# A chunked scan: the triangular inverse built from pairs X and U = X Aᵀ, one 128-column product per level

## What is computed

```python
def wkv_scan(state, r, w, k, v, a, b, reverse):
    def step(s, inp):
        r_t, w_t, k_t, v_t, a_t, b_t = inp
        sa = jnp.einsum('bhij,bhj->bhi', s, a_t)
        s = s * w_t[:, :, None, :] + sa[..., None] * b_t[:, :, None, :] + v_t[..., None] * k_t[:, :, None, :]
        return s, jnp.einsum('bhij,bhj->bhi', s, r_t)
```

## Time and profile before

| | |
|---|---|
| median of 3 runs | 2158.53 us (2154.55 to 2166.66) |
| profiled execution, its own time | 2158.71 us |
| its span in the profile | 2156.9 us |
| PE busy over the span | 1983.1 us |
| scan, about | 1190 to 2010 us of the span |
| PE busy in that stretch | 718.85 of 820 us |
| DVE, ACT, POOL busy in that stretch | 519.94, 345.90, 325.01 us |

### The profile page before, as it was taken

One profiled execution on the slowest core, in us unless ns is written; L12 is line 12 of the kernel. 1 busy time (PEld: TensorE's weight loads), 2 busy tenths in 40 slices (PEclk: granted clock), 3 DMA queues, 4 the chain that ended last, 5 costly groups with the idle time before them and its releaser, 6 DMA issues. The chain is left out here.

```text
span 2156.9 us, 64929 instructions
## 1 busy us (share of the span) xinstructions
PE 1983.1 (92%) x28556; PEld 1318.3 (61%) x28556; DVE 1120.8 (52%) x2187; ACT 701.5 (33%) x1985; POOL 541.3 (25%) x669
## 2 busy tenths in 40 slices
PE   6999999999999999999898788888889888988698
PEld 3556556344444454544343688888888888888443
DVE  4534333124756592042442566656666666766684
ACT  4111111133335642221012344344444444444332
POOL 1011010013113430002111433334434343434011
PEclk9999999999999999999999899999999999999899
DMA  8200000811016767546432333443333333332742
GB/s 345 103 20 25 34 20 20 347 63 49 22 55 167 203 176 206 154 151 202 156 112 80 96 84 92 127 115 85 98 86 100 87 96 88 100 99 64 242 135 100
DMA packets 269820, 248.24 MB, mean 115 GB/s; under 512 B 92770, under 2 KB 226146, under 8 KB 266083
## 3 DMA queue, kind: packets, MB, share of 16 engines
q1 hardware_dynamic: 269538, 244.09, 37.2%
HBM read 164.32 MB, written 79.69 MB: 113 GB/s over the span
## 5 line engine op out<-in xcount | busy, mean ns | idle before, releaser
L2173 PE MATMUL ps<-M,AT 64*64 64x64 f32 x6400 | 278.6, 222 | 37.3 <-issue 32.2
L1019 PE MATMUL ps<-xt,w_slab 128*128 128x512 f32 (+1 forms) x800 | 297.5, 525 | 0.0
L2173 PEld LDWEIGHTS ps<-M,AT 64*64 64x64 f32 x6400 | 234.7, 136 | 49.8 <-issue 37.8
L2173 PE MATMUL ps<-TT,MT 64*64 64x64 f32 x5120 | 223.7, 222 | 23.9 <-issue 21.6
L1019 PEld LDWEIGHTS ps<-xt,w_slab 128*128 128x128 f32 x800 | 148.3, 190 | 146.3 <-issue 122.6
L2173 PEld LDWEIGHTS ps<-TT,MT 64*64 64x64 f32 x5120 | 195.5, 136 | 29.6 <-issue 25.6
L2037 DVE COPY_PREDICATED TT<-mask,ps 128x128 f32<-128x128 int32 x400 | 130.2, 325 | 149.4 <-PE ps L2173 141.3
L1905 POOL TENSOR_TENSOR bk<-feat,growth 128x256 f32<-128x256 f32 x160 | 117.2, 754 | 348.2 <-ACT growth L1950 348.2
L2163 PE MATMUL ps<-ar,bk 64*64 64x192 f32 (+1 forms) x1280 | 133.2, 320 | 20.8 <-POOL ar L1915 14.3
L645 PE MATMUL ps<-h,fgo 128*128 128x512 f32 x320 | 142.7, 600 | 2.4 <-PEq L202 2.4
L2166 PE MATMUL ps<-ar,bk 64*64 64x192 f32 (+1 forms) x1280 | 134.1, 327 | 1.2 <-issue 1.2
(11 more groups left out here) (299 smaller groups left out, 4060.3 us busy)
## 6 DMA issues: line engine op xcount, KB each, us to landing
feat<-feature_scratch SPq DMA_DIRECT2D x160, 256.0 KB
feature_scratch<-k_feats SPq DMA_DIRECT2D x64, 320.0 KB, 5.1
feature_scratch<-k_feats SPq DMA_DIRECT2D x24, 640.0 KB, 6.8
k_feats<-in_modw SPq DMA_DIRECT2D x8, 1536.0 KB, 6.7
w_slab<-in_rwin SPq DMA_DIRECT2D x24, 512.0 KB, 6.6
V<-v_token_scratch SPq DMA_DIRECT2D x320, 32.0 KB, 2.6
fgo<-in_modw SPq DMA_DIRECT2D x8, 1024.0 KB, 8.7
fw_slab<-in_fwin SPq DMA_DIRECT2D x16, 512.0 KB, 4.5
```

The source lines that it names most:

```text
L1019: mm = pe.matmul(ps[:, bank, 0:n], (w1t if i is None else w[:, i % 2])[:, k, :], src[:, k, a:a + n], start=k == 0, stop=k == KT - 1)
L2173: mm = pe.matmul(out[o, b, :], L[o, b, :], R[o, b, :], start=True, stop=True)
```

## The change

The levels now carry two matrices side by side in one tile (`XU`, and `XU1` for the first chunk stage): X, the transposed inverse so far, and U = X Aᵀ. DVE masks the U half of the PSUM bank into `W[k]` and transposes W; PE then multiplies that once with the pair [X, U], 128 columns for each block and head (`u1`, then `l2`, `l4`, `l8`). At k = 16 only X is carried (64 columns), and level 32 is done with two rounds as before (`t32`, `mt32`). That makes seven rounds in place of ten: u1, l16, t32 and mt32 of 64 columns, l2, l4 and l8 of 128. ACT copies back the whole bank (512 columns) after l2 and l4, the 256 columns of U after u1, and changed halves after l8, l16 and mt32. The masks' and transposes' order on DVE, ACT's order and PE's order are rewritten; some buffers exist once instead of twice. DMA issues and POOL's work stay.

```diff
-PA = {"g0": 1, "g1": 2, "t2": 3, "m2": 4, "t4": 5}
-PB = {"m4": 1, "t8": 2, "m8": 3, "t16": 4, "m16": 5, "t32": 6, "mt32": 7}
+PA = {"g0": 1, "g1": 2, "u1": 3, "l2": 4}
+PB = {"l4": 1, "l8": 2, "l16": 3, "t32": 4, "mt32": 5}
...
-            def second(j, cc, name):
-                act.wait_ge(pb, count("second", j, cc, PB["mt32" if name == "xt" else name]))
...
+            def first_u1(j, cc):
+                act.wait_ge(da, count("dve_first", j, cc, DA["w2"]))
+                act.activation(flat(XU1[:, 1]), ps[:, 4, 256:512], ACT.Copy).then_inc(aa, 1)
+
+            def second_xu(j, cc, k):
+                act.wait_ge(db, count("dve_second", j, cc, DB[f"w{2 * k}"]))
+                act.activation(xcols(par(cc)), ps[:, 4 if k == 2 else 5, :], ACT.Copy).then_inc(ab, 1)
...
+            def second_x(j, cc, k, done):
+                act.wait_ge(pb, count("second", j, cc, PB[done]))
+                act.activation(changed(xcols(par(cc)), k), changed(ps[:, 5, :], k), ACT.Copy).then_inc(ab, 1)
...
-            def second_t(j, cc, k):
-                v.wait_ge(pb, count("second", j, cc, PB[f"t{k}"]))
-                masked(k, cc, 5).then_inc(db, 1)
-
-            def second_mt(j, cc, k):
-                v.wait_ge(ab, count("act_second", j, cc, AB[f"m{k}"]))
-                v.transpose(flat(MT[trd(j, cc)][:]), flat(M[par(cc)])).then_inc(db, 1)
...
+            def second_tt(j, cc, k):
+                v.wait_ge(db, count("dve_second", j, cc, DB[f"w{k}"]))
+                v.transpose(flat(TT_second[:]), W_cols[k][:, 0:256]).then_inc(db, 1)
+
+            def second_m16(j, cc):
+                v.wait_ge(ab, count("act_second", j, cc, AB["l16"]))
+                v.transpose(flat(M16[:]), xcols(par(cc))[:, 0:256]).then_inc(db, 1)
...
+            def l2(j, cc):
+                pe.wait_ge(da, count("dve_first", j, cc, DA["tt2"]))
+                pe.wait_ge(aa, count("act_first", j, cc, AA["u1"]))
+                for b in range(B4):
+                    for h in two:
+                        o = own(h)
+                        mm = pe.matmul(lev(4)[o, :, b, :], TT_first[o, b, :], XU1[o, :, b, :], start=True, stop=True)
+                mm.then_inc(pa, 1)
+
+            def l(j, cc, k):
                 s = par(cc)
-                pe.wait_ge(da, count("dve_first", j, cc, DA["m1"]))
-                ge(pe, da, count("dve_first", j, cc - 1, DA["t4"]))
-                level(lev(4), AT[s], M[s], pa)
-
-            def m2(j, cc):
+                pe.wait_ge(db, count("dve_second", j, cc, DB[f"tt{k}"]))
+                pe.wait_ge(ab, count("act_second", j, cc, AB[f"l{k // 2}"]))
+                if k == 4:
+                    ge(pe, ab, count("act_second", j, cc - 1, AB["xt"]))
+                x = slice(0, 2 if k < 16 else 1)
+                for b in range(B4):
+                    for h in two:
+                        o = own(h)
+                        mm = pe.matmul(lev(5)[o, x, b, :], TT_second[o, b, :], XU[s][o, x, b, :], start=True, stop=True)
+                mm.then_inc(pb, 1)
...
             def period(j, c, ahead):
...
                 if A_:
-                    t2(j, a)
+                    l2(j, a)
                 if B_:
-                    m(j, b, 16)
+                    t32(j, b)
                 if Q_:
                     b_state(j, c, 1)
-                if A_:
-                    m2(j, a)
-                if B_:
-                    t(j, b, 32)
                 if lat:
                     y(j, c, 1)
-                if A_:
-                    t4(j, a)
                 if B_:
                     mt32(j, b)
```

More of the change, by code:

```diff
@@ L1731, in scan @@
     AT = [sb(f"AT{s}", [P, B4, CK]) for s in two]
[L1732 to L1735, removed]
+    XU1 = sb("first_XU", [P, 2, B4, CK])
+    XU = [sb(f"XU{s}", [P, 2, B4, CK]) for s in two]
+    M1, M16, TT_first, TT_second = (sb(n, [P, B4, CK]) for n in ("M1", "M16", "TT_first", "TT_second"))
+    W_cols = {k: sb(f"W{k}", [P, B4 * CK + 2 * k]) for k in LEVELS}
     blocks = lambda t: t[:, 0:B4 * CK].rearrange("p (b t) -> p b t", b=B4)
-    M, TT = [blocks(t) for t in M_cols], {k: [blocks(t) for t in TT_cols[k]] for k in LEVELS}
+    W = {k: blocks(W_cols[k]) for k in LEVELS}
     Rs = [sb(f"R{s}", [P, NDIR, CK]) for s in two]
@@ L1936, in _, with identities @@
             act.wait_ge(tab_in, 16)
[L1938 to L1942, removed]
+            def identities():
+                for e in [XU1[:, 0]] + [W[k] for k in LEVELS]:
+                    act.activation(e, ident.unsqueeze(1).broadcast_to([P, B4, CK]), ACT.Copy).then_inc(msk, 1)
+            identities()
             def exps(j, cc):
@@ L2012, in period @@
                 if B_:
[L2013 removed]
+                    second_x(j, c + 1, 32, "mt32")
             for j in range(KT):
@@ L2167, in products, with u1 @@
                 mm.then_inc(pa, 1)
-            def level(out, L, R, done):
+            def u1(j, cc):
+                s = par(cc)
+                pe.wait_ge(da, count("dve_first", j, cc, DA["m1"]))
+                ge(pe, ab, count("act_second", j, cc - 1, AB["l2"]))
                 for b in range(B4):
@@ L2203, in m @@
[L2203 to L2206, removed]
+                        mm = pe.matmul(lev(4)[o, 1, b, :], M1[o, b, :], AT[s][o, b, :], start=True, stop=True)
+                mm.then_inc(pa, 1)
[6 more added lines that the diff above has]
+                        mm = pe.matmul(lev(4)[o, :, b, :], TT_first[o, b, :], XU1[o, :, b, :], start=True, stop=True)
+                mm.then_inc(pa, 1)
@@ L2208, in mt32, with t32 @@
+            def t32(j, cc):
+                s = par(cc)
+                pe.wait_ge(db, count("dve_second", j, cc, DB["m16"]))
+                for b in range(B4):
+                    for h in two:
+                        o = own(h)
+                        mm = pe.matmul(lev(5)[o, 1, b, :], AT[s][o, pos(b), :], M16[o, pos(b), :], start=True, stop=True)
+                mm.then_inc(pb, 1)
             def mt32(j, cc):
@@ L2210, in mt32 @@
                 pe.wait_ge(db, count("dve_second", j, cc, DB["t32"]))
-                level(lev(5), TT[32][s], MT[trd(j, cc)], pb)
+                for b in range(B4):
+                    for h in two:
+                        o = own(h)
+                        mm = pe.matmul(lev(5)[o, 0, pos(b), :], W[32][o, b, :], XU[s][o, 0, pos(b), :], start=True, stop=True)
+                mm.then_inc(pb, 1)
             def at(sub, d):
```

165 lines of the change are left out of this document (76 added, 89 removed).

## The result

The changed kernel takes 2091.94 us (median of 4 runs, 2083.88 to 2096.16) against 2159.05 us; the ratio is 0.968, with an interval of 0.964 to 0.972. That is 67 us less. The forecast was 2105, with a range of 2055 to 2150.

What follows compares the result with a forecast made beforehand. The prediction took PE's late instruction code, about as much as columns, to bound the scan: 9.2 us of work and waits plus 0.24 of gaps, taken as 9.4 for 10.06, over 80 periods saves 53 us: 2105 us, range 2055 to 2150.

Steps and rivals of the forecast that it cites:

- The bound: Scan on PE: instruction blocks arrive each 4.2 us against 3.34 us of work per block, so PE runs out of code.
- the 8.43 of work: PE's own work in a latent period of the old scan, in us, said to be borne out by the shortest period.
- PE's rounds: Scan's level rounds on PE: four of 64 and three of 128 columns take 4.50 us for 4.65, 0.15 less a period.
- The packets: PE's instruction queue in the scan: 48 fewer matmul rows a period bring 195 blocks down to 165.
- The walk: One latent period followed step by step: 8.28 us of PE work plus 0.85 to 0.9 of waits, 9.2 in all.
- the 60 to 70 us of named waits: PE in the scan: waits on ACT's XU copy at l4 and DVE's M at u1, replacing waits named issue.
- The 0.1 that was taken off for lighter context periods: Scan's mean period: context periods, two in ten, have smaller products and no y, so 0.1 us less.
- What is left of the gaps: PE's waits for code after the change: 19 us over the scan, 0.24 a period, with blocks of 4.28 us.
- 1 (less wait than walked): Scan: waits smaller than walked and blocks coming at their own pace, giving 2032 to 2074 us; chance 0.15.
- 2: Scan on PE: only columns count, new waits vanish but gaps stay, 12 us less, 2147 us; chance 0.08.
- 4: Scan: long copies or a handover chain hold PE 1.7 us or more, giving 2155 to 2175 us; chance 0.1.
- 3: Scan: new waits add to code gaps, period 10.45 to 10.7 us, time 2190 to 2210 us; chance 0.1.

Runs made afterwards that it cites:

- e1: Changed kernel with each 128-column matmul of l2, l4 and l8 issued as two of 64 columns, same results: 2181.24 us, 1.010 of the kernel before.
- e2: Changed kernel with only l8's 128-column matmuls issued as two of 64 columns: 2117.97 us, 0.980 of the kernel before.
- e4: Kernel before the change with rounds t2 and m2 issued at 128 columns, same number of instructions: 2169.75 us, 1.004 of the kernel before.
- e9: Changed kernel with l16, t32 and mt32 multiplying only the 32 of 64 columns read afterwards: 2090.32 us, 0.967 of the kernel before.
- e5: Changed kernel with PE's u1 behind a_state 1 and r_state 1, and DVE's state add ahead of the first mask: 2103.37 us, 0.972 of the kernel before.
- e8: Kernel before the change with t8, m8, t16, m16 and t32 multiplying only the 32 columns read afterwards: 2167.12 us, 1.002 of the kernel before.

## Why the prediction was right

The change gained 67 us where 53 were forecast, and by the step that carried the forecast: fewer instructions, and so fewer waits for code. That the number came within 13 us is in part luck, for two terms were off in opposite directions. The steps one by one:

**The bound.** PE waits for its instructions, block by block. e1, e2 and e4 show it, from both sides: instructions without columns cost 89 us (e1), columns without instructions 7 to 9 (e4). And each gap of the kernel before ends 1.06 to 1.62 us after a packet of code. The page's rule that was weighed against it (the Trainium skill, Runtime: NRT & Kernel Launch, Instruction fetch mechanics: fetching hidden by the issue pace) does not hold for this kernel; gaps of 0.16 to 2.36 us went and came with the number of instructions. One reading of the prediction does not hold: the period of 8.53 us that was to bear out the 8.43 of work is one of context, for ACT copies no Y in it, and by the prediction's own steps it has about 1.0 us less of work. The 8.43 hold all the same: summed over the starts of PE's rows between 1212 and 1930 us, it stood still for about 1.8 us a period (an estimate from the trace), 1.3 of them in the listed gaps, which leaves 8.3 of work in the mean of latent and context periods.

**PE's rounds.** The 128-column round took 0.89 us (0.88 said), its upper bound of 0.93 was not needed. That the 64-column rounds had little less to give was not known: by e9 half the columns take 0.44 us in place of 0.465. The three rounds of double width, 0.89 each, take 0.12 us less than six of 0.465 (0.15 said), and 48 matmul rows go with them: nearly all of the gain lies in the rows.

**The packets.** 166 in place of 165.

**The walk.** This was the mis-sized term: 9.2 us for a period with code always there, measured 8.80 (the median of the 47 periods without a listed gap; the shortest have 8.76), so 0.4 too much. PE's own work by the measured rounds is 8.31, so the waits are 0.5 us a period and not 0.85 to 0.9. The head of the latent period whose end stands above, PE's timeline from 1556.1 to 1561 (mt32, products, l4):

```profile
1556.20 0.68 PE L2230 MATMUL ps<-XU,W 64*64 64x64 f32 x16
1556.78 0.38 PE L2177 MATMUL ps<-ar,bk 64*64 64x192 f32 x2
1557.80 0.98 PE L2212 MATMUL ps<-XU,TT_second 64*64 64x128 f32 x14
```

The products start 0.58 after mt32, whose length is 0.465: a wait of 0.12 that the walk did not have. l4 starts 1.02 after them, where PE was free at 0.89: a wait of 0.13, for 0.28 said. Counted from mt32, l4 comes at 1.60, and the walk has 0.465 + 1.17 = 1.64: it was right in when, and split the wait wrongly. u1 comes at 5.10 (1561.30), and the walk has 5.50; it waits 0.13, for 0.42 said. From u1 on the walk is right: mt32 follows 3.70 later (1565.00), with 0.13 of wait, as said. So the whole 0.4 lies ahead of u1. Each of the four waits is 0.12 to 0.13 us, too short for a list that starts at 0.15: together some 0.5 us a period and 40 us over the scan, which is why the 60 to 70 us of named waits were not found there. Context periods, which have no y and less work on PE, are as long (8.78): u1 waits 0.34 us in them. So once code is there, it is the chain of handovers that sets the changed kernel's pace, and not the sum of PE's work.

What went another way ahead of u1 is the chunk's first mask, 0.25 of the 0.4:

```profile
L2051 DVE COPY_PREDICATED first_XU<-mask,AT 128x256 f32<-128x256 int32 x80 | 36.0, 450 | 51.2 <-ACT NG L1953 51.2
```

0.45 us in place of 0.70. In the older kernel that copy (L2049) took 0.44 to 1.01 us, and its trace shows when. 55 of the 80 started with more than 0.17 us left of an operation on POOL, and each of them ended 0.30 to 0.32 us after that operation's end, whether 0.18 or 0.70 us of it were left. The other 25 took 0.44 to 0.48, also where POOL's next operation ran beside them. In the changed kernel POOL starts after that mask:

```profile
1308.92 1.42 POOL L1903 TENSOR_TENSOR bk<-feat,growth 128x256 f32<-128x256 f32 x2 [4.29 <-ACT growth L1948]
```

```profile
1308.27 0.45 DVE L2051 COPY_PREDICATED first_XU<-mask,AT 128x256 f32<-128x256 int32 x1 [0.61 <-ACT NG L1953]
1308.76 0.45 DVE L2055 STREAM_TRANSPOSE M<-first_XU 128x256 f32<-128x256 f32 x1
```

The mask ends at 1308.72, POOL's bk begins at 1308.92. So the mean of 0.70 that the walk took held a wait for POOL that the new order does not have; the two traces show this, no run was made to change the order alone. Another 0.1 was gained up to the end of the NG copy that the mask waits for: the 512-column copy took 0.59 us (0.67 said), and ACT as a whole 394 / 80 = 4.9 us a period in place of 5.6. The last 0.05 lies between M's transpose and u1. The 0.1 that was taken off for lighter context periods, and the 0.1 put on against it, had neither of them a ground.

```profile
L1961 ACT ACTIVATE XU<-ps 128x512 f32<-128x512 f32 x160 | 94.7, 592 | 5.2 <-DVE W L2039 5.2
```

**What is left of the gaps.** Said were 0.24 us a period with blocks of 4.28 us, measured 9.22 - 8.80 = 0.42 (of which 0.28 are listed gaps). With the shorter waits a block lasts 8.80 x 126.6 / 272 = 4.10 us, and more of the tail shows. The two errors have opposite signs, -0.4 and +0.2, and leave 9.22 for 9.4: 14 us, the whole difference between 2105 and 2092.

**The rivals.** 1 (less wait than walked) had a part of the truth, as 8.80 for 9.2 tells. 2 is refuted by e1 and e4, 4 by the XU copy's 0.59 us and waits of 0.5 us a period. 3, that waits add to the gaps in place of covering them, did not decide the change, but e1 shows it at work: there gaps of 1.05 us a period and the new waits stand side by side, and the kernel is 1% slower than before. The change pays because it takes the instructions away with the rounds; its structure alone loses. (The chance given for a time below 2147.7 is a slip of addition: 0.57, 0.15 and 0.04 make 0.76 and not 0.79.)

Handing over to ACT and DVE in the changed kernel leaves PE little slack. e5 moved one wait and got a longer one, and none of the kernels that compute the whole beats the changed one by more than can be told (e9: 0.967 against 0.968).

## What to carry to other kernels

Where matmuls are small and code is written out, count PE's instructions as a resource of its own: set the packets of PE's instruction queue against the stretch, and compare the time of one block's work with the pace at which blocks come (here 3.3 us against some 4). Gaps in the middle of a run of matmuls that wait for no semaphore, at even distances in instructions, are its mark. Where a block's work is shorter than that pace, fewer and wider instructions gain, and more columns cost little (e4); that fewer columns gain nothing there is likely but not shown, for e8's narrow rounds were hardly shorter. Where it is longer, waits of other engines cost again, and the data transfers that delay code are the next thing to look at.

## What the runs showed of the hardware

- Code for PE came as 16 KB packets, one for 126 to 127 matmul rows and as many weight loads. PE went on 1.06 to 1.62 us after a packet's end where it had run out of code. From a block's start to the next block's code there passed, by the estimate above, 3.9 to 4.0 us in the median and 4.9 at the 90th percentile, 4.5 without the feature loads.
- A round of eight fp32 64x64 matmuls took 0.44 us at 32 columns, 0.465 at 64 and 0.88 to 0.90 at 128 (0.92 in e4).
- A masked copy of runs of two elements took 0.40 to 0.45 us, of longer runs 0.30 (same 128 columns); a 512-column copy out of PSUM on ACT 0.59 us.
- A masked copy of 256 columns from one SBUF tile to another took 0.45 us alone; where it started during a POOL operation it ended 0.30 to 0.32 us after that operation's end (55 of 80, kernel before).
- Columns added in the old kernel's rounds (e4) were nearly free: 66 us of work for 7 to 9 us of time.
